# Other places in SBUF for the expert weights and the transposed rows of a hybrid decoder layer

## What is computed

```python
def expert_block(args):
    xblk, e = args
    hdn = jax.nn.silu(xblk @ w_gate[e]) * (xblk @ w_up[e])   # 128 x 1024 by 1024 x 512, twice
    return hdn @ w_down[e]                                   # 128 x 512 by 512 x 1024
```

## Time and profile before

| | |
|---|---|
| median of 3 executions | 1137.91 us (1136.37 to 1139.71) |
| profiled execution, first to last instruction | 1136.3 us; its own time outside this span is not in the profile |
| PE busy | 98% of the span |
| DVE, ACT, POOL busy | 70%, 55%, 19% |
| mean granted clock of TensorE | 0.991 of full speed |
| bytes moved by DMA | 288.31 MB |

### The profile page before, as it was taken

How to read it: one execution, slowest core, us unless ns; L and a number is a source line. 1 busy time by engine, 2 the same in 40 slices (tenths; PEclk the granted TensorE clock), 3 DMA queues, 4 the chain that set the end, 5 groups by cost and what they waited for, 6 DMA issues and landing times.

```text
span 1136.3 us, 15447 instructions
## 1 busy us (share of the span) xinstructions
PE 1109.4 (98%) x5435; PEld 909.1 (80%) x5435; DVE 798.8 (70%) x1123; ACT 625.1 (55%) x694; POOL 211.7 (19%) x186
## 2 busy tenths in 40 slices
PE   8999999999999999999999999999999999999986
PEld 7878889778888787877888888888888888888852
DVE  3310233135455787779999999988999889998787
ACT  4311313213434410036878888788887888878644
POOL 3000111100000000002334322242423324233110
PEclk9999999999999999999999999999999999999998
DMA  7513314631211521248999999999999999999875
GB/s 281 202 57 121 121 46 123 208 96 38 75 40 52 190 78 54 93 153 340 409 378 361 404 381 385 395 380 386 384 388 369 381 395 376 390 383 387 314 316 222
DMA packets 69160, 288.31 MB, mean 254 GB/s; under 512 B 16229, under 2 KB 20325, under 8 KB 43508
## 3 DMA queue, kind: packets, MB, share of 16 engines
q1 hardware_dynamic: 56112, 258.34, 59.9%
q0 software_dynamic: 11840, 25.09, 6.0%
q10 hardware_dynamic: 1156, 4.20, 0.9%
HBM read 266.66 MB, written 37.75 MB: 268 GB/s over the span
## 4 chain that ended last, share of the span: by engine, by line
PE 93%; DVE 3%; DMA 2%; issue 1%; ACT 1%; DVEq 0%; POOL 0%; POOLq 0%; ACTq 0%
PE bank L1643 26%; PE bank L1645 25%; PE bank L1644 25%; PE bank L2020 2%; PE bank L2120 1%; PE bank L2055 1%; PE bank L1858 1%; PE bank L1860 1%; PE bank L1863 1%; PE bank L1907 1%; DMA expert_rows<-yt,dix 1%; PE bank L1657 1%; PE bank L1816 1%; PE bank L1872 1%; PE bank L1899 1%
## 5 line engine op out<-in xcount | busy, mean ns | idle before, releaser
L1643 PE MATMUL bank<-whi,xghi 128*128 128x512 f32 x512 | 203.2, 397 | 1.0 <-DVE xglo L1487 1.0
L1645 PE MATMUL bank<-whi,xglo 128*128 128x512 f32 x512 | 200.6, 392 | 0.0
L1644 PE MATMUL bank<-wlo,xghi 128*128 128x512 f32 x512 | 199.9, 390 | 0.0
L1474 DVE TENSOR_TENSOR wlo<-raw_down,whi 128x2048 fp32r<-128x2048 f32 x64 | 146.3, 2291 | 28.0 <-ACT whi L816 27.9
L1643 PE MATMUL bank<-whi,xhi 128*128 128x512 f32 x384 | 156.9, 409 | 1.5 <-DVE wlo L996 0.7
L1644 PE MATMUL bank<-wlo,xhi 128*128 128x512 f32 x384 | 151.9, 396 | 0.0
L1645 PE MATMUL bank<-whi,xlo 128*128 128x512 f32 x384 | 151.6, 395 | 0.0
L1474 DVE TENSOR_TENSOR wlo<-raw,whi 128x2048 fp32r<-128x2048 f32 x64 | 146.4, 2289 | 4.1 <-ACT whi L816 3.2
L1474 DVE TENSOR_TENSOR wlo<-raw_up,whi 128x2048 fp32r<-128x2048 f32 x64 | 146.3, 2285 | 0.0
L816 ACT ACTIVATE whi<-raw_up 128x2048 fp32r<-128x2048 f32 x64 | 122.5, 1915 | 25.8 <-PE bank L1645 25.4
L816 ACT ACTIVATE whi<-raw_down 128x2048 fp32r<-128x2048 f32 x64 | 122.4, 1912 | 23.7 <-PE bank L1645 23.7
(11 more groups left out here) (344 smaller groups left out, 1733.1 us busy)
## 6 DMA issues: line engine op xcount, KB each, us to landing
raw<-l_w_gate SPq DMA_DIRECT2D x64, 1024.0 KB, 8.5
raw_up<-l_w_up SPq DMA_DIRECT2D x64, 1024.0 KB, 8.4
raw_down<-l_w_down SPq DMA_DIRECT2D x64, 1024.0 KB, 8.2
raw<-l_w_in SPq DMA_DIRECT2D x5, 2048.0 KB, 10.1
yy<-expert_rows SPq DMA_DIRECT2D x8, 1024.0 KB, 7.9
xt<-hcat SPq DMA_DIRECT2D x8, 512.0 KB, 4.1
o_rows<-stage POOLq DMA_DIRECT2D x16, 256.0 KB, 2.5
qkT<-qk_rows SPq DMA_DIRECT2D x16, 256.0 KB, 3.8
```

What stands on the lines that cost most here:

```text
L1474: tt(wlo[k][:, halves(p)], raw_e[k][:, halves(p)], whi[k][:, halves(p)].bitcast(F32), ALU.subtract).then_inc(e_lo[k], 1)
L1643: t.matmul(out, lh, rh, start=first, stop=False)
L1644: t.matmul(out, lh, rl, start=False, stop=False)
L1645: return t.matmul(out, ll, rh, start=False, stop=last)
```

## The change

It puts tiles at other addresses, and makes the zero block narrower.

```diff
+LINE = 512
+GATE_PLACE, UP_PLACE, DOWN_PLACE, ROWS_PLACE, HIDDEN_PLACE = 0, 128, 256, 64, 64
...
-    whi = [at(f"whi{s}", [P, PIECE], F32R) for s in range(2)]
-    wlo = [at(f"wlo{s}", [P, PIECE], F32R) for s in range(2)]
+    def begin_at(place):
+        cursor[0] += (place - cursor[0]) % LINE
+
+    begin_at(GATE_PLACE)
+    whi = [at("whi0", [P, PIECE], F32R)]
+    wlo = [at("wlo0", [P, PIECE], F32R)]
+    begin_at(UP_PLACE)
+    whi.append(at("whi1", [P, PIECE], F32R))
+    wlo.append(at("wlo1", [P, PIECE], F32R))
...
     cursor[0] = x_at
+    begin_at(DOWN_PLACE)
     whi.append(at("whi2", [P, PIECE], F32R))
     wlo.append(at("wlo2", [P, PIECE], F32R))
...
     xg = [at(f"xg{i}", [P, D]) for i in range(2)]
+    begin_at(ROWS_PLACE)
     xghi = [at(f"xghi{i}", [P, KC, P], F32R) for i in range(2)]
     xglo = [at(f"xglo{i}", [P, KC, P], F32R) for i in range(2)]
     sg = at("sg", [P, FE])
     gu = at("gu", [P, FE])
+    begin_at(HIDDEN_PLACE)
     ghi = at("ghi", [P, FC, P], F32R)
...
-    clear = over("r_kn", "clear", [P, 256])
+    clear = over("r_kn", "clear", [P, 128])
...
-            sp.dma_start(ys[...].rearrange("(p a) (r c) -> p (a r) c", a=2, c=256), clear[:].unsqueeze(1).to_broadcast([P, 8, 256])).then_inc(rows_landed[n], 16)
+            sp.dma_start(ys[...].rearrange("(p a) (r c) -> p (a r) c", a=2, c=128), clear[:].unsqueeze(1).to_broadcast([P, 16, 128])).then_inc(rows_landed[n], 16)
```

More of the change, by code:

```diff
@@ L144, in build @@
     ftmp = at("ftmp", [P, NT])
-    slots = cursor[0]
-    whi = [at(f"whi{s}", [P, PIECE], F32R) for s in range(2)]
-    wlo = [at(f"wlo{s}", [P, PIECE], F32R) for s in range(2)]
+    def begin_at(place):
[6 more added lines that the diff above has]
+    wlo.append(at("wlo1", [P, PIECE], F32R))
     x_at = cursor[0]
@@ L432, in _ @@
         for n in range(EARLY):
-            sp.dma_start(ys[2 * TOKEN_TILE[n] * P:2 * (TOKEN_TILE[n] + 1) * P, :].rearrange("(p a) (r c) -> p (a r) c", a=2, c=256), clear[:].unsqueeze(1).to_broadcast([P, 8, 256])).then_inc(rows_landed[n], 16)
+            sp.dma_start(ys[2 * TOKEN_TILE[n] * P:2 * (TOKEN_TILE[n] + 1) * P, :].rearrange("(p a) (r c) -> p (a r) c", a=2, c=128), clear[:].unsqueeze(1).to_broadcast([P, 16, 128])).then_inc(rows_landed[n], 16)
         sp.wait_ge(N["lo_done"], lo_count(5))
```

## The result

| | before | after |
|---|---|---|
| median of 4 executions each | 1138.35 us (1136.37 to 1139.71) | 1145.85 us (1144.94 to 1147.25) |
| profiled execution, span | 1136.3 us | 1144.0 us |

What follows compares the result with a forecast made beforehand. The prediction took PE's matmul pace to bound the kernel. Its terms, 0 + 8.8 + 0 + 0 = +8.8 us on the median of 1137.9, gave 1146.7 us; likeliest case 1142 to 1150, overall 1120 to 1150.

Steps and rivals of the forecast that it cites:

- What bounds the kernel: Whole kernel: PE is busy 98% of the span, so time is the number of matmuls times their pace.
- Places of the expert stage: Expert stage: new differences lose the settled 226.6 ns; 54 matmuls x 5.1 ns x 32 items, +8.8 us.
- the 18 matmuls that the forecast left as they are: Expert item: the slower, unsettled matmuls, behind transposes or just before them, taken as unchanged.
- The upper bound of +11.6 us: Expert stage: 54 matmuls at the slowest trio's pace, 6.7 ns more each, over 32 items.
- The row that carried the choice: `gate_rows`, 384 columns, difference kept at -64: 174.5 ns each, read as 4.5 ns above a settled 170.0.
- The first rival: Expert stage: the new differences settle as well, no change, 1137.9 us, within 1135 to 1141; chance 0.27.
- The other side: Expert stage: operand streams stop holding each other up; 1109.8 us in full, 1124 at half; chance 0.31.
- Early stages: Stages ahead of the experts: the difference still runs through all multiples of 64, mean stays 231.7 ns, 0 us.
- ACT, DVE, DMA: Their tiles move by multiples of 64 bytes; no dependence seen and PE hides any loss, 0 us.
- The zero block: Its DMAs get twice the pieces, SP's issue perhaps 5.93 us more, hidden, 0 us; rival 12 us once, 2 in 100.

Runs made afterwards that it cites:

- e4: The changed kernel with all weights at 0 and the rows at 64, difference +64 everywhere: 1148.88 us, ratio 1.0101 to the kernel before.
- e5: Matmuls alone, as e1, with finer steps, fewer columns and other types: reduced float32 233.33 ns at +64, bf16 215.83 at 0 and 64 alike.
- e8: Matmuls alone, as e1, with places moving on, other orders and other starts: 226.67 ns fixed, 231.67 with either or both operands stepping 64 bytes a chunk.
- e1: A kernel of its own, matmuls alone at 28 pairs of places, nothing else running: 226.67 ns at difference 0, 233.33 at +64.
- e3: The changed kernel with all five places at 64, difference 0 again: 1135.83 us against 1137.52 for the kernel before, ratio 0.9988.

## Why the prediction was right

**What bounds the kernel.** Right. In every kernel above PE's waits kept their size (the longest, at the end, 4.2 to 5.3 us) and the time followed PE's pace.

**Places of the expert stage, +8.8 us.** Right in where the time goes (PE's pace falls by the places alone, for as long as a stretch lasts) and in its sum; that the sum fits so closely is in part luck, for its terms are off in both directions. The forecast had 54 matmuls an item at 231.7, with an item of 18.05 us; measured are 18.06 us and 31 x 0.287 = 8.9 us. But the 5.1 ns came from stages that are slow for another reason (below), and the changed kernel has two values: +64 settles at 233.3 (+6.7 ns) and -64 at 228.9 (+2.3). Of the 54 the 24 of up have -64 and 30 have +64: 24 x 2.3 + 30 x 6.7 = 256 ns, where 275 were forecast. The other 31 of the 287 ns fall on the 18 matmuls that the forecast left as they are, 1.7 ns each. The "231 to 233 ns" forecast for down and up together holds only on average: down 233.5, up 228.8. The upper bound of +11.6 us was in truth a value that a different choice of places gets close to: e4 has 1.0101, +11.4 us.

**The row that carried the choice.** The nearest row was the earlier trace rows, read as "a kept difference of -64 stays 4.5 ns above the settled pace of 170.0". e5 shows this reading to be wrong. The settled pace of 384 columns is 173.33, not 226.6 x 384/512 = 170.0, since part of a matmul's time does not shrink with the columns: the 128 columns from 384 to 512 cost 53.3 ns, and four times that leaves 13.3 ns of the 226.67. And a stationary operand of 32 columns has 230.25 to 231.67 ns at 0 and the three multiples of 64 tried, no better at 0. Besides, both operands of `gate_rows` move on by 64 bytes at each chunk, which in e8 is slow even at difference 0. So `gate_rows`, with 8 and 16 columns, says nothing on the difference. The chance of 0.42 for this case stood on it; the early stages were the sound argument, and they say only that drifting places are slow.

**The first rival, the new differences settle.** They do settle, but not at 226.6: each difference has its own lasting pace, 233.3 at +64 and 228.9 at -64. The forecast's idea that PE "loses the settled state" should read: it settles elsewhere. The early stages are slow for another reason, as e8 shows: one of their operands moves on by 64 bytes from each chunk to the next, and every such drift in e8 gives their 231.67.

**The other side, the streams are freed.** Wrong: with nothing else running no difference tried is under 226.67. Its size rested on the earlier trace rows, two passes in 428.8 ns. e5 shows one plain float32 matmul as two records of 429.17 each, so what one record passes is not settled by this row. The floor near 215 is real all the same, for another type: 215.83 ns in bf16. The Trainium skill, page "TensorE: Matmul & The Clock Gate", section "Back-to-back issue gap", gives N/2.4 + 2.5 ns, 215.8 for 512 columns, as the gap of an isolated matmul, which the prediction left out. bf16 agrees with the formula even back to back, and reduced float32 has 10.8 ns more at its best. For a sustained stream the same section of the Trainium skill gives about 131 ns at 512 columns; no run here comes near that, the lowest is 215.83. By the Trainium skill, page "SBUF — State Buffer", section "Who interferes with whom", PE's two reads are independent and PE waits on no one, from which the prediction took 0 us for the places; e1 against that rule has 226.67 to 234.17 ns by the places alone, with no other engine at work.

**Early stages, 0.** Right, 231.7 before and after the earlier trace rows; e8 gives the same 231.67 for each of the five drifts run.

**ACT, DVE, DMA, 0.** Right: in e3 all of these tiles lie elsewhere than before too, and it is not slower.

**The zero block, 0.** Right, and its size too: SP's issue was to take 5.93 us more and took 5.5. The transfers themselves did not take twice as long: the median to landing is 9.9 us, before 9.2. The prediction said that `w_out`'s weights are used after 400 us; their first use is ACT's split (L661), at 363.6 us in the trace of before, which changes nothing at an issue of 221.45.

**What stays open.** Why reduced float32 costs 10.8 ns over bf16 at its best, and what lets a match modulo 256 bytes keep step, is not shown: only that it is between PE's two operand streams, and that difference 0 gives a gain for reduced float32 with 128 stationary columns and none for bf16, plain float32 or 32 stationary columns. What chooses between the two states at -16 in the kernel is open too. Not tried: giving the early stages repeated places. Some 1300 matmuls x 5.0 ns (231.67 - 226.67) = 6.5 us is what it could bring, an estimate that takes all of them to the settled pace; rows of the input padded from 4160 to 4608 bytes would repeat modulo 512, and whether there is room for them was not tried.

## What to carry to other kernels

If reduced-float32 matmuls bound a kernel, and their stationary operands are 128 columns wide, let the moving and the stationary operand begin at the same place modulo 256 bytes, and let every chunk keep it (here the chunks are 2048 and 512 bytes long; a step of 64 more costs 5 ns a matmul). Here that is worth up to 1.0% of the whole kernel (e4), and of the places tried none was faster than the same place. Read such things as the distance from start to start over some 24 matmuls: the busy time of a matmul was 0.39 to 0.40 us in fast and slow places alike. When a row is used as the nearest likeness, check that it is alike in what might matter (here the number of stationary columns), or the right number comes out of the wrong row.

## What was not expected of the hardware

- The pace depends on the places of the two operands within 256 bytes: 226.67 ns at difference 0, 228.9 at -64, 231.9 to 234.2 at +32 to +160, and 232.33 as soon as the difference is 4 bytes.
- At -16 bytes the place counts too: 226.67 or 228.33 ns with moving at 0 (the first behind an even number of short matmuls, the second behind an odd one, in the cases 1 to 8 that were run alone), 228.33 with moving at 64, 231.67 with moving at 16. In the kernel down has 228.3 behind 8 transposes.
- With both operands drifting together by 64 bytes a chunk, the difference always 0, the pace is 231.67.
- The number of matmuls that start 427 ns apart (1.2 GHz) differs from trace to trace, 0 to 15 in the eight traces of the whole kernel.
